# Rope keys padded to 128 rows and a bf16 mask product in the latent-attention scores of a two-block layer stack

## The chip, the cores and the metric

The kernel runs on one core of a Trainium2 chip. The metric is the time of one execution on the device, in microseconds (us). The engines are named as in the profile: PE is TensorE's matmul, PEld its weight load, DVE is VectorE, ACT is ScalarE, POOL is GpSimd, SP is SyncE, which issues DMAs here.

## What is computed

Two model blocks follow one another on 512 tokens of width 1024. The first has two layers: gated linear attention with a SwiGLU feed-forward, then latent attention (MLA) with another SwiGLU. The second block has pooling and convolution branches and a mixture of single-neuron experts. The change lies in the MLA layer, whose scores are

```
s = (einsum('bqhd,bkhd->bhqk', qn_b, k_nope)
     + einsum('bqhd,bkd->bhqk', qr_b, k_rope)).astype(float32) * scale
mask = kpos[None, :] <= qpos[:, None]
p = softmax(where(mask, s, -inf), axis=-1)
o = einsum('bhqk,bkhd->bqhd', p, v)
```

There are 8 heads, 128 non-rope and 64 rope dimensions, a value width of 128, and 4 blocks of 128 queries. The rope key `k_rope` is one for all heads. Everything is float32.

## The kernel before

The engines' programs are written out by hand and tied by semaphores; each engine runs its own list in order. Weights come from memory in blocks through a ring of four (`raw`, then ACT copies them into `w_hi`, L566, then POOL makes the rest `w_lo`, L548), and a dense product is three single-pass products of such parts. Stages run one after the other; PE's order is `pe_program`, and the MLA stage is `pe_mla`.

Within the MLA stage the latent projections come first, then the projections for queries, keys and values, then the score loop, then the output projection `mla_out` by dense products. The queries' rope parts are in `m_qr`, [128 partitions, 4, 512]: two heads share one slot, the even head in partitions 0 to 63, the odd one in 64 to 127. The rotated key `m_kr`, [128, 512], holds the same 64 rows twice, once in each half. DVE makes it at L1364 to L1366 (`kr_done`), long ahead of the score loop: ACT waits for `kr_done` at L822 before it writes `m_sw` again, and PE waits for it at L1881.

The score loop runs over s = 0 to 31, four steps for a head, with a query block `qb` = s % 4. Step s computes scores for n = 128 (qb + 1) keys, so 128, 256, 384 and 512 columns in turn:

- PE: three products accumulate in one bank `pa[:, s % 3]`: the non-rope part (L1890, `m_qn` by `m_kn`, 128 rows), the rope part (L1891, `m_qr` by `m_kr`, the 64 rows of the head's half), and the causal mask of the diagonal 128 columns (L1892, the identity by a table `causal_t` of 0 and -1e30). All operands are float32; one float32 product shows in the trace as two MATMUL records. Then come the transposes of the probabilities of step s - 2 (L1899), and once in a head, at qb = 2, the product of the transposed probabilities with the values of the head before (`m_PT` by `m_v`, eight records), "PV" below.
- DVE: the row maximum of step s (L1381), its scaling (L1382), then for step s - 1 the reciprocal of the sum (L1386) and the scaling of `m_P` (L1388, `at_n`), on which the transposes wait; once in a head `h_lo` (L1392).
- ACT: the exponential of step s (L854, `at_p`), the copy of the transposed probabilities of step s - 2 (L861, `at_To`), once in a head `h_hi` (L867).

PE's product helper is `mm` at L1623, so products of many stages have that one line in the profile and are told apart by their operands; the mask product is the one with `consts` alone. SP has loaded three blocks for `mla_out` before the loop starts, and `mla_out` waits for the last `h_lo` (L1910).

Of the kernel before, what the change touches and what calls it, by code (L numbers as in the profile page):

```python
# [24 lines left out]
BF16 = mybir.dt.bfloat16  # L25
U32 = mybir.dt.uint32
I32 = mybir.dt.int32
ALU = mybir.AluOpType
# [3 lines left out]
P = 128  # L32
S = 512
# [12 lines left out]
MH, NOPE, ROPE, MVD = 8, 128, 64, 128  # L46
# [101 lines left out]
def two_blocks(nc, A, out):  # L148
# [11 lines left out]
    def at(name, offset, shape, dt=F32):  # L160
        return nc.alloc_sbuf_tensor_at(name, [P] + shape, dt, offset=base + offset)

    K = 1024
# [14 lines left out]
    rstd_off = misc  # L178
    rstd = at("rstd", misc, [S])
    misc += 2 * K  # L180
    ada_off = misc
# [13 lines left out]
    def ar(name, offset, shape, dt=F32):  # L195
        n = int(np.prod(shape)) * (2 if dt == BF16 else 4)
        assert offset + n <= arena_bytes, (name, offset + n, arena_bytes)
        return at(name, AR + offset, shape, dt)
# [34 lines left out]
    m_qr = ar("m_qr", 16 * K, [MH // 2, S])  # L233
    m_kn = ar("m_kn", 24 * K, [MH, S])
    m_v = ar("m_v", 40 * K, [TT, MH * MVD])
    m_kr = ar("m_kr", 56 * K, [S])
    m_cos = ar("m_cos", 58 * K, [S])
    m_sin = ar("m_sin", 60 * K, [S])
    m_c = ar("m_c", 62 * K, [5, S])
    m_kraw = ar("m_kraw", 72 * K, [S])  # L240
    m_sw = ar("m_sw", 74 * K, [S])
    m_t = ar("m_t", 76 * K, [S])
# [5 lines left out]
    c_lo = ar("c_lo", 82 * K, [5, S], F32R)  # L248
    c_hi = at("c_hi", ada_off, [5, S], F32R)
    m_st = at("m_st", ada_off + 10 * K, [MH * TT, 4])  # L250

    ssq = ar("ssq", 0, [DT, S])
    s_a1 = ar("s_a1", 0, [4, S])
# [54 lines left out]
    pa = nc.alloc_psum_tensor("pa", [P, 4, 512], F32)  # L308
# [6 lines left out]
    def const(name, n, rows=P):  # L315
        return consts[0:rows, CONST[name]:CONST[name] + n]

    ident, ones = const("ident", P), const("ones", P)
# [34 lines left out]
    k_raw, sw_done, qr_done, kr_done = sem("k_raw"), sem("sw_done"), sem("qr_done"), sem("kr_done")  # L353
# [416 lines left out]
    def act_mla(act, hi):  # L770
# [42 lines left out]
        for t in range(12):  # L813
            m = M0["mla_q"] + t // 2
            hi.upto(m + 3)
            act.wait_ge(blk_done, m + 1)
            bank = ps[:, (T + t) % RING, :]
            if t < MH:
                nc.scalar.activation(m_qn[:, t, :], bank, ACT.Copy).then_inc(tile_free, 1)
            else:  # L820
                j = t - MH
                act.wait_ge(kr_done, 1)  # L822
                if j >= 2:
                    act.wait_ge(qr_done, j - 1)
                dst = (m_sw, m_kraw)[j % 2]
                for q in range(4):
                    nc.scalar.activation(dst[32 * q:32 * q + 32, :], bank[32 * (q ^ 1):32 * (q ^ 1) + 32, :], ACT.Copy)\
                      .then_inc(sw_done, 1)
# [502 lines left out]
    def dve_mla(dve):  # L1331
        def step(ins):
            own_d.link(dve, ins)

        v = nc.vector

        dve.wait_ge(ld_v[2], 16)
        step(v.tensor_copy(m_ang[:, :], m_pos[:, :]))
        step(v.tensor_scalar(m_ang[:, :], m_ang[:, :], const("freq", 1), None, ALU.mult))
        step(v.tensor_scalar(m_t[:, :], m_ang[:, :], 1.0 / TWO_PI, MAGIC, ALU.mult, ALU.add))  # L1340
        step(v.tensor_scalar(m_t[:, :], m_t[:, :], -MAGIC, None, ALU.add))
        for c in (C1, C2, C3):
            step(v.scalar_tensor_tensor(out=m_ang[:, :], in0=m_t[:, :], scalar=-c, in1=m_ang[:, :], op0=ALU.mult, op1=ALU.add))

        step(v.tensor_scalar(m_t[:, :], m_ang[:, :], np.pi / 2, None, ALU.add))
        step(v.tensor_scalar(m_cos[:, :], m_t[:, :], PI_BELOW, -TWO_PI, ALU.is_gt, ALU.mult))
        step(v.tensor_tensor(m_t[:, :], m_t[:, :], m_cos[:, :], ALU.add))
        step(v.tensor_scalar(m_t[:, :], m_t[:, :], PI_BELOW, -PI_BELOW, ALU.min, ALU.max))
        v.tensor_scalar(m_ang[:, :], m_ang[:, :], PI_BELOW, -PI_BELOW, ALU.min, ALU.max).then_inc(ang_done, 1)

        dve.wait_ge(trig_done, 1)
        for a, tiles in enumerate((range(0, 3), range(3, 5))):
            dve.wait_ge(c_rs, a + 1)
            for t in tiles:
                g = col("mla_g_q", t) if t < 3 else col("mla_g_kv", t - 3)
                v.scalar_tensor_tensor(out=m_c[:, t, :], in0=m_c[:, t, :], scalar=g, in1=m_rs[:, a, :],
                                       op0=ALU.mult, op1=ALU.mult).then_inc(c_t, 1)
            for t in tiles:
                dve.wait_ge(c_h, t + 1)
                v.tensor_tensor(c_lo[:, t, :], m_c[:, t, :], c_hi[:, t, :].bitcast(F32), ALU.subtract).then_inc(c_rd, 1)  # L1360

        dve.wait_ge(trig_done, 1)
        dve.wait_ge(tile_free, T0["mla_qn"])
        step(v.tensor_tensor(m_kr[:, :], m_kraw[:, :], m_cos[:, :], ALU.mult))  # L1364
        step(v.tensor_tensor(m_sw[:, :], m_sw[:, :], m_sin[:, :], ALU.mult))
        v.tensor_tensor(m_kr[:, :], m_kr[:, :], m_sw[:, :], ALU.add).then_inc(kr_done, 1)  # L1366
        T = T0["mla_qr"]
        for j in range(MH // 2):
            dve.wait_ge(blk_done, M0["mla_q"] + 4 + j // 2 + 1)
            dve.wait_ge(sw_done, 4 * (j + 1))  # L1370
            sw = (m_sw, m_kraw)[j % 2]
            v.tensor_tensor(m_qr[:, j, :], m_cos[:, :], ps[:, (T + j) % RING, :], ALU.mult).then_inc(tile_free, 1)
            step(v.tensor_tensor(sw[:, :], sw[:, :], m_sin[:, :], ALU.mult))
            dve.wait_ge(tile_free, T + j + 1)
            v.tensor_tensor(m_qr[:, j, :], m_qr[:, j, :], sw[:, :], ALU.add).then_inc(qr_done, 1)

        n_it = MH * TT
        for s in range(n_it + 4):
            if s < n_it:
                dve.wait_ge(at_s, s + 1)  # L1380
                step(v.tensor_reduce(m_st[:, s, 0:1], pa[:, s % 3, 0:P * (s % TT + 1)], AX.X, ALU.max))  # L1381
                v.tensor_scalar(m_st[:, s, 1:2], m_st[:, s, 0:1], -MSCALE, None, ALU.mult).then_inc(at_m, 1)  # L1382
            if 1 <= s <= n_it:
                r = s - 1
                dve.wait_ge(at_p, s)
                step(v.reciprocal(m_st[:, r, 3:4], m_st[:, r, 2:3]))  # L1386
                pr = m_P[:, r % 2, 0:P * (r % TT + 1)]
                v.tensor_scalar(pr, pr, m_st[:, r, 3:4], None, ALU.mult).then_inc(at_n, 1)  # L1388
            if s >= 7 and (s - 7) % TT == 0:
                h = (s - 7) // TT  # L1390
                dve.wait_ge(at_oh, h + 1)
                v.tensor_tensor(h_lo[:, h, :], ps[:, 2 + h % 2, :], h_hi[:, h, :].bitcast(F32), ALU.subtract).then_inc(at_ol, 1)  # L1392
        dve_residual(dve, "mla_out", 1, 2, 3)
# [228 lines left out]
    def mm(out, a, b, start, stop_):  # L1622
        return nc.tensor.matmul(out, a, b, start=start, stop=stop_)  # L1623
# [209 lines left out]
    def pe_mla(pe):  # L1833
# [44 lines left out]

        pe.wait_ge(tile_free, T0["mla_out"])
        pe.wait_ge(qr_done, MH // 2)  # L1880
        pe.wait_ge(kr_done, 1)  # L1881
        n_it = MH * TT
        for s in range(n_it + 3):
            if s < n_it:
                h, qb = divmod(s, TT)
                if s >= 3:
                    pe.wait_ge(at_p, s - 2)
                n, q = P * (qb + 1), slice(qb * P, (qb + 1) * P)
                half = slice(ROPE * (h % 2), ROPE * (h % 2 + 1))
                mm(pa[:, s % 3, 0:n], m_qn[:, h, q], m_kn[:, h, 0:n], True, False)  # L1890
                mm(pa[:, s % 3, 0:n], m_qr[half, h // 2, q], m_kr[half, 0:n], False, False)  # L1891
                mm(pa[:, s % 3, n - P:n], ident, const("causal_t", P), False, True).then_inc(at_s, 1)  # L1892
            if 2 <= s < n_it + 2:
                r = s - 2
                pe.wait_ge(at_n, r + 1)
                if r >= 2:
                    pe.wait_ge(at_To, r - 1)
                for kb in range(r % TT + 1):
                    last = nc.tensor.transpose(ps[:, r % 2, kb * P:(kb + 1) * P], m_P[:, r % 2, kb * P:(kb + 1) * P], ident)  # L1899
                last.then_inc(at_T, 1)  # L1900
            if s >= 6 and (s - 6) % TT == 0:
                h = (s - 6) // TT
                pe.wait_ge(at_To, TT * (h + 1))
                if h >= 2:
                    pe.wait_ge(at_ol, h - 1)
                for kb in range(TT):
                    last = mm(ps[:, 2 + h % 2, kb * P:S], m_v[:, kb, h * MVD:(h + 1) * MVD], m_PT[:, h % 2, kb, kb * P:S],
                              kb == 0, kb == TT - 1)
                last.then_inc(at_o, 1)
# [251 lines left out]
```

## Time and profile before

| | us |
|---|---|
| median of 3 runs | 3251.67 (3250.89 to 3251.94) |
| the profiled execution, its own time | 3249.77 |
| its span, first to last instruction | 3247.7 |
| PE busy | 3108.9 (96%) |
| POOL, DVE, ACT busy | 1771, 1606, 1152 |
| score loop, first score product to the first `mla_out` product | 808.98 to 903.73 |

```text
span 3247.7 us, 44125 instructions
## 1 busy us (share of the span) xinstructions
PE 3108.9 (96%) x14602; PEld 2502.0 (77%) x14602; DVE 1605.6 (49%) x2785; ACT 1151.8 (35%) x1478; POOL 1771.1 (55%) x2040
## 2 busy tenths in 40 slices
PE   5988999999999999997999999999999999999998
PEld 3777788876578887775788888888888788888886
DVE  7873454322435551694407996444411444444443
ACT  4354322236332213433323325555543322232222
POOL 3833677645047766573455665444446665566663
PEclk8989999999999999998999999999999999999999
DMA  7511455423025553221233444555564655555652
GB/s 304 207 36 61 151 186 191 153 71 96 1 78 200 187 187 112 87 88 61 85 98 112 146 136 169 184 184 184 188 240 141 217 200 186 179 169 196 202 191 72
DMA packets 170201, 481.94 MB, mean 148 GB/s; under 512 B 15360, under 2 KB 48896, under 8 KB 168080
## 3 DMA queue, kind: packets, MB, share of 16 engines
q1 hardware_dynamic: 147680, 410.83, 38.8%
q10 hardware_dynamic: 22448, 70.14, 5.6%
q8 instruction: 46, 0.75, 0.1%
q14 instruction: 27, 0.22, 0.0%
HBM read 411.70 MB, written 69.21 MB: 148 GB/s over the span
## 4 chain that ended last, share of the span: by engine, by line
PE 56%; issue 21%; POOL 19%; DVE 2%; ACT 1%; DMA 0%; DVEq 0%; POOLq 0%; SPq 0%; ACTq 0%
PE ps L1623 52%; POOL w_lo L548 19%; PE pa L1623 3%; DVE s_acc L1417 1%; DMA e_g<-expert_act 0%; DVEq L1414 0%; DVE s_pb L1429 0%; DVE s_tmp L1468 0%; DVE mg_lo L1470 0%; ACT mg_hi L918 0%; DVE s_m L1466 0%; DVE x L1122 0%; ACT L614 0%; POOLq L546 0%; POOLq L552 0%
## 5 line engine op out<-in xcount | busy, mean ns | idle before, releaser
L548 POOL TENSOR_TENSOR w_lo<-raw,w_hi 128x256 fp32r<-128x256 f32 x2036 | 1770.9, 902 | 1446.4 <-ACT w_hi L566 1444.5
L1623 PE MATMUL ps<-h_hi,w_hi 128*128 128x512 f32 x2392 | 950.2, 397 | 43.2 <-POOL w_lo L548 19.6
L1623 PE MATMUL ps<-h_hi,w_lo 128*128 128x512 f32 x2392 | 939.7, 393 | 0.0
L1623 PE MATMUL ps<-h_lo,w_hi 128*128 128x512 f32 x2392 | 915.7, 390 | 0.0
L566 ACT ACTIVATE w_hi<-raw 128x1024 fp32r<-128x1024 f32 x509 | 538.8, 1060 | 844.4 <-PE ps L1623 727.9
L1623 PEld LDWEIGHTS ps<-h_hi,w_hi 128*128 128x128 f32 x2392 | 454.9, 190 | 145.2 <-issue 25.9
L1623 PEld LDWEIGHTS ps<-h_hi,w_lo 128*128 128x128 f32 x2392 | 454.6, 190 | 95.3
L1623 PEld LDWEIGHTS ps<-h_lo,w_hi 128*128 128x128 f32 x2392 | 450.3, 188 | 93.3 <-issue 1.7
L1623 PE MATMUL ps<-wa_hi,w_lo 128*128 128x512 f32 x1024 | 408.6, 399 | 0.0
L1623 PE MATMUL ps<-wa_lo,w_hi 128*128 128x512 f32 x1024 | 403.5, 394 | 0.0
L1623 PE MATMUL ps<-wa_hi,w_hi 128*128 128x512 f32 x1024 | 401.5, 392 | 0.3 <-DVE x L1587 0.3
L1069 DVE CUSTOM_DVE_ANT_0 ada<-ada,cvec 128x1024 f32<-128x1024 f32 x144 | 228.5, 1625 | 32.1 <-DMA ada<-in_ada 27.9
L1623 PEld LDWEIGHTS ps<-wa_lo,w_hi 128*128 128x128 f32 x1024 | 192.2, 188 | 50.1
L1623 PEld LDWEIGHTS ps<-wa_hi,w_hi 128*128 128x128 f32 x1024 | 192.2, 188 | 46.5 <-DVE x L1587 0.7
L1623 PEld LDWEIGHTS ps<-wa_hi,w_lo 128*128 128x128 f32 x1024 | 192.2, 188 | 44.2
L1580 DVE TENSOR_TENSOR wa_lo<-e_t,wa_hi 128x512 fp32r<-128x512 f32 x128 | 137.5, 1074 | 152.6 <-ACT wa_hi L1005 152.6
L925 ACT ACTIVATE g_act<-ps 128x512 f32<-128x512 f32 x128 | 76.6, 598 | 348.9 <-PE ps L1623 348.9
L1577 DVE TENSOR_TENSOR e_t<-e_g,e_w 128x512 f32<-128x512 f32 x128 | 108.5, 848 | 165.1 <-DMA e_g<-expert_act 164.4
L1587 DVE SCALAR_TENSOR_TENSOR x<-ps,mod,x 128x512 f32<-128x512 f32 x128 | 95.7, 748 | 183.7 <-PE ps L1623 183.6
L1005 ACT ACTIVATE wa_hi<-e_t 128x512 fp32r<-128x512 f32 x128 | 80.8, 631 | 207.2 <-DVE e_t L1577 207.2
L1552 DVE TENSOR_TENSOR oh_hit<-iota_t,r_key 128x1024 bf16<-128x1024 bf16 x64 | 46.5, 726 | 215.5 <-PE pa L1623 215.1
L985 ACT ACTIVATE w_st<-pa 128x512 f32<-128x512 f32 x128 | 134.2, 1160 | 39.3 <-PE pa L1623 30.5
(315 smaller groups left out, 3088.7 us busy)
## 6 DMA issues: line engine op xcount, KB each, us to landing
ada<-in_ada SPq DMA_DIRECT2D x144, 512.0 KB, 4.4
raw<-in_expert_u SPq DMA_DIRECT2D x128, 512.0 KB, 4.1
raw<-in_expert_v SPq DMA_DIRECT2D x128, 512.0 KB, 4.2
raw<-in_ffn_in SPq DMA_DIRECT2D x88, 512.0 KB, 3.5
expert_act<-g_act ACTq DMA_DIRECT2D x128, 256.0 KB, 4.3
gate_matrix<-w_st ACTq DMA_DIRECT2D x16, 2048.0 KB, 6.7
e_w<-gate_matrix SPq DMA_DIRECT2D x16, 2048.0 KB, 11.2
e_g<-expert_act SPq DMA_DIRECT2D x128, 256.0 KB, 7.8
```

What stands on the lines that cost most here:

```text
L548: last = nc.gpsimd.tensor_tensor(w_lo[:, k, c:c + 256], raw[:, k, c:c + 256], w_hi[:, k, c:c + 256].bitcast(F32), ALU.subtract)
L566: nc.scalar.activation(w_hi[:, k, :], raw[:, k, :], ACT.Copy).then_inc(hi_done, 1)
L925: nc.scalar.activation(g_act[:, k % 2, :], ps[:, (T + k) % RING, :], ACT.Gelu_apprx_tanh)\
L985: nc.scalar.activation(w_st[:, b, :, 4 * q:4 * q + 4].rearrange("p n t -> p t n"), pa[:, q % 4, :].rearrange("p (t n) -> p t n", t=4), ACT ...
L1005: nc.scalar.activation(wa_hi[:, b, k, :], e_t[:, :], ACT.Copy).then_inc(wa_h, 1)
L1069: return nc.vector.tensor_tensor_reduce(out=w, in0=w, in1=cvec[:, :], scale=1.0, scalar=0.0, op0=ALU.mult, op1=ALU.add, accum_out=dst).the ...
L1417: v.scalar_tensor_tensor(out=s_acc[:, t, :], in0=s_gl[:, t, bass.ds(i + 1, S)], scalar=cols[:, bass.ds(i + (COLS["dw_kernel"] + t * CK + 1 ...
L1552: v.tensor_tensor(oh_hit[:, b, :, :, :], column, key1, ALU.is_equal).then_inc(oh_hits, 1)
L1577: v.tensor_tensor(e_t[:, :].rearrange("p (t k) -> p t k", k=WTOK), e_g[:, k % 4, :].rearrange("p (t k) -> p t k", k=WTOK), e_w[:, :, k, :] ...
L1580: v.tensor_tensor(wa_lo[:, b, k, :], e_t[:, :], wa_hi[:, b, k, :].bitcast(F32), ALU.subtract).then_inc(wa_done, 1)
L1587: v.scalar_tensor_tensor(out=x[:, k, :], in0=ps[:, (T + k) % RING, :], scalar=mod[:, GATE[6] + k:GATE[6] + k + 1], in1=x[:, k, :], op0=ALU ...
L1623: return nc.tensor.matmul(out, a, b, start=start, stop=stop_)
```

## The change

`m_kr` becomes two tensors, one for the even and one for the odd heads. Each has the rotated key in the 64 partitions of its heads and zeros in the other 64. The second lies where `rstd` lies, which is free in this stage. The rope product then takes all 128 rows of `m_qr`: the other head's rows meet zeros. The identity and the mask table are copied once to bf16 (0 and 1 are exact, and -1e30 stays as good as minus infinity), into unused bytes beside `m_st`, and the mask product uses these. DVE now issues two multiplications, two memsets, two half-height additions and two casts where it issued two multiplications and one addition, and `kr_done` counts six of them; ACT at L822 and PE at L1881 wait for all six.

```diff
-    m_kr = ar("m_kr", 56 * K, [S])
+    m_kr = [ar("m_kr0", 56 * K, [S]), at("m_kr1", rstd_off, [S])]
...
+    ident_b = at("ident_b", ada_off + 10 * K + 512, [P], BF16)
+    causal_b = at("causal_b", ada_off + 10 * K + 768, [P], BF16)
...
-                act.wait_ge(kr_done, 1)
+                act.wait_ge(kr_done, 6)
...
-        step(v.tensor_tensor(m_kr[:, :], m_kraw[:, :], m_cos[:, :], ALU.mult))
+        step(v.tensor_tensor(m_t[:, :], m_kraw[:, :], m_cos[:, :], ALU.mult))
         step(v.tensor_tensor(m_sw[:, :], m_sw[:, :], m_sin[:, :], ALU.mult))
-        v.tensor_tensor(m_kr[:, :], m_kr[:, :], m_sw[:, :], ALU.add).then_inc(kr_done, 1)
+        for a in range(2):
+            mine, other = slice(ROPE * a, ROPE * (a + 1)), slice(ROPE * (1 - a), ROPE * (2 - a))
+            v.memset(m_kr[a][other, :], 0.0).then_inc(kr_done, 1)
+            v.tensor_tensor(m_kr[a][mine, :], m_t[mine, :], m_sw[mine, :], ALU.add).then_inc(kr_done, 1)
+        v.tensor_copy(ident_b[:, :], ident).then_inc(kr_done, 1)
+        v.tensor_copy(causal_b[:, :], const("causal_t", P)).then_inc(kr_done, 1)
...
-        pe.wait_ge(kr_done, 1)
+        pe.wait_ge(kr_done, 6)
...
-                half = slice(ROPE * (h % 2), ROPE * (h % 2 + 1))
                 mm(pa[:, s % 3, 0:n], m_qn[:, h, q], m_kn[:, h, 0:n], True, False)
-                mm(pa[:, s % 3, 0:n], m_qr[half, h // 2, q], m_kr[half, 0:n], False, False)
-                mm(pa[:, s % 3, n - P:n], ident, const("causal_t", P), False, True).then_inc(at_s, 1)
+                mm(pa[:, s % 3, 0:n], m_qr[:, h // 2, q], m_kr[h % 2][:, 0:n], False, False)
+                mm(pa[:, s % 3, n - P:n], ident_b[:, :], causal_b[:, :], False, True).then_inc(at_s, 1)
```

## Rows read from the trace of the kernel before

**Rows 1.** Windows: stretch; its length, then PE, PEld, DVE, ACT, POOL busy, clock.

```profile
779.00:782.40 3.40, 1.84 (x7) 1.05 (x6) 2.26 (x4) 3.28 (x6) 2.69 (x4) 1.00 0.02 5
809.80:820.00 10.20, 10.20 (x20) 4.49 (x19) 2.52 (x10) 1.86 (x7) 0.00 (x0) 0.50 0.01 2
894.00:898.40 4.40, 1.79 (x12) 1.07 (x11) 2.49 (x7) 2.14 (x5) 0.00 (x0) 1.00 0.00 0
898.40:902.00 3.60, 3.60 (x7) 1.83 (x7) 0.00 (x0) 0.00 (x0) 0.00 (x0) 0.53 0.00 0
```

**Rows 2.** Timeline, PE alone, in one head: start, us, line, product, count, idle before.

```profile
828.87 1.02 PE L1623 MATMUL pa<-m_kn,m_qn 128*128 128x512 f32 x2
829.82 1.12 PE L1623 MATMUL pa<-m_kr,m_qr 64*128 64x512 f32 x2
830.88 0.49 PE L1623 MATMUL pa<-consts 128*128 128x128 f32 x2
831.20 0.38 PE L1899 MATMUL ps<-consts,m_P 128*128 128x128 f32 x2
831.42 0.39 PE L1623 MATMUL pa<-m_kn,m_qn 128*128 128x128 f32 x2
831.74 0.48 PE L1623 MATMUL pa<-m_kr,m_qr 64*128 64x128 f32 x2
832.15 0.49 PE L1623 MATMUL pa<-consts 128*128 128x128 f32 x2
832.87 0.55 PE L1899 MATMUL ps<-consts,m_P 128*128 128x128 f32 x3 [0.23 <-DVE m_P L1388]
833.25 0.60 PE L1623 MATMUL pa<-m_kn,m_qn 128*128 128x256 f32 x2
...
834.73 0.60 PE L1899 MATMUL ps<-consts,m_P 128*128 128x128 f32 x4
...
837.18 2.32 PE L1623 MATMUL ps<-m_PT,m_v 128*128 128x512 f32 x8
839.34 0.59 PE L1623 MATMUL pa<-m_kn,m_qn 128*128 128x512 f32 x1
```

**Rows 3.** Timeline of the same head, DVE and ACT.

```profile
831.40 0.69 DVE L1381 TENSOR_REDUCE m_st<-pa 128x1 f32<-128x512 f32 x1 [3.39 <-PE pa L1623]
...
832.39 0.42 DVE L1388 TENSOR_SCALAR m_P<-m_P,m_st 128x384 f32<-128x384 f32 x1
...
833.90 0.49 DVE L1388 TENSOR_SCALAR m_P<-m_P,m_st 128x512 f32<-128x512 f32 x1
...
836.04 0.59 ACT L861 ACTIVATE m_PT<-ps 128x512 f32<-128x512 f32 x1
```

**Rows 4.** Timeline, PE alone, in the expert stage, where bf16 products stand between others.

```profile
1999.94 1.55 PE L1623 MATMUL pa<-oh_gate,oh_key 128*128 128x128 bf16 x24
2001.29 0.48 PE L1623 MATMUL ps<-h_hi,w_hi 128*128 128x512 f32 x1
2001.61 0.39 PE L1623 MATMUL ps<-h_lo,w_hi 128*128 128x512 f32 x1
2001.84 0.40 PE L1623 MATMUL ps<-h_hi,w_lo 128*128 128x512 f32 x1
```

**Rows 5.** Timeline, DVE alone, around `m_kr`, and a memset from the groups by line.

```profile
761.61 1.12 DVE L1366 TENSOR_TENSOR m_kr<-m_kr,m_sw 128x512 f32<-128x512 f32 x1
776.20 0.69 DVE L1372 TENSOR_TENSOR m_qr<-m_cos,ps 128x512 f32<-128x512 f32 x1 [13.47 <-ACT m_sw L827]
...
L1157 DVE MEMSET g_attn<- 128x2048 f32 x1 | 1.8, 1765 | 1.2 <-PEq L2156 1.2
```

**Rows 6.** Timeline, PE alone, start of the loop and its last PV.

```profile
810.48 1.06 PE L1623 MATMUL pa<-m_kn,m_qn 128*128 128x256 f32 x2
...
813.20 1.49 PE L1623 MATMUL pa<-m_kn,m_qn 128*128 128x384 f32 x2
...
898.20 4.12 PE L1623 MATMUL ps<-m_PT,m_v 128*128 128x512 f32 x8 [0.69 <-ACT m_PT L861]
```

## The prediction

> **What bounds the kernel now.** The page comes first: PE is busy 96% of the span and no other engine above 55%, so the time is PE's list and the gaps in it. The change touches only the score loop of the MLA stage, 808.98 to 903.73, so I read the views of that stretch. The timeline of PE alone over one head [rows 2] shows a head period of 10.47 us (828.87 to 839.34) with one visible wait, the 0.23 us before the transposes of the 384-column step; those wait for DVE's scaling of `m_P`. The reader should see that PE's list fills the head, and that DVE's chain comes just behind it at one place. The windows [rows 1] show the second thing: from 809.8 to 820 TensorE was granted its lower level, 1.2 GHz (clock 0.50), though PE has work without a break. The third view, DVE alone ahead of the loop [rows 5], tells whether the added DVE work has room.
>
> **The rope product.** The yardstick is PV in [rows 2]: eight records over 2560 columns take 837.18 to 839.34, 2.16 us, so 0.84 ns for a column of a record when one 128-row float32 product follows another. By it the two records of the non-rope product and the two of the rope product cost 4 x 128 x 0.84 = 0.43 us for 128 columns, 0.86 for 256, 1.30 for 384 and 1.73 for 512. Measured from the first product to the transposes, or to the end of the mask product at its 0.32 us: the 512-column step 828.87 to 831.20, 2.33; the 128-column step 831.42 to 832.15 plus 0.32, 1.05; the 256-column step 833.25 to 834.73, 1.48 [rows 2]. The excess is 0.60, 0.62 and 0.62 us, independent of the columns, so I take 0.61 for 384 columns as well. Within it the mask product is two records of 128 columns, 0.22 at the yardstick. The other 0.39 us stands at the two borders of the rope product (64 rows between 128 and 128): it takes 1.06 us where the non-rope one with the same columns takes 0.95, and 0.41 against 0.32. Streaming 128 rows in place of 64 costs nothing, as columns are what is counted: 512 columns cost 1.06 us even with 64 rows.
>
> The Trainium skill's page TensorEngine Tiling, section Key Properties, says that a change of tiling mode drains the engine. By that rule the borders are the cause and vanish with equal heights; the page gives no price. Were the rule wrong here, the 0.39 us would belong to every change of weights, and rival B would hold; PV in [rows 2], which changes weights for every column block with no such gap, speaks for the rule.
>
> **The mask product.** In bf16 it is one record of 128 columns. Twenty-four such products take 1999.94 to 2001.29, 1.35 us, 0.06 each [rows 4]. At the return to other operands one product takes 0.32 where the next takes 0.23 (2001.29, 2001.61, 2001.84), 0.09 more. So the mask product costs between 0.06 and 0.15 us; the trace has none in a float32 group. I take 0.12, nearer the upper end, since each is alone between float32 work here. **PE's list thus shrinks by 0.61 - 0.12 = 0.49 us a step,** 15.7 over 32 steps if nothing else bound it.
>
> **What DVE's chain takes back, in one head.** (1) After the 512-column step. Now: mask product 830.88, maximum from 831.40, scaling of the 384 columns 832.39 for 0.42, transposes 832.87 [rows 2, 3]; 1.99 us from mask to transposes, in which PE works 0.32 + 0.22 + 1.05 = 1.59. With the mask product 0.20 shorter the chain starts 0.20 sooner and takes 1.79; PE's work is 0.12 + 0.22 + 0.55 = 0.89 and PE waits 0.9. Gain 0.20, not 0.69. (2) The next transposes come 1.86 us later (832.87 to 834.73), and DVE is ready at 833.90 + 0.49 + 0.05 = 834.44, 1.57 after. PE's work falls to 0.38 + 0.86 + 0.12 = 1.36, so the chain decides: gain 0.29. (3) From there to PV now 2.45 us (834.73 to 837.18); 0.49 less is 1.96, while PV needs ACT's copy, 836.04 + 0.59 = 836.63, 1.90 after [rows 3]. That just holds: gain 0.49. (4) PV and the first two products of the 512-column step: gain 0.60 - 0.32 = 0.28. Sum 1.26 us a head, and the period goes from 10.47 to 9.21.
>
> **First head, last head.** At 1.2 GHz the 256-column step takes 810.48 to 813.20, 2.72 us [rows 6]; at twice the yardstick it would be 1.72 + 0.2, so the gain is 0.8, and over the first three steps and the 512-column step up to its mask about 2.7. Seven periods follow: 7 x 1.26 = 8.8. The last mask product gives 0.2; behind it the chain of waits to the first `mla_out` product, 10 us, is untouched. Sum 11.7. As head 1 begins sooner, more of it falls into the slow clock if that ends at 820 as now, which returns about 0.6: **11.1 us with the slow stretch as it is.**
>
> **The clock.** The slow stretch at the loop's start lasts 10.2 us; the one at the last PV, all of 128 rows, is over by 902, after 3.6 us, though both have PE busy throughout [rows 1]. What stands in the first and not in the second are the 64-row products, nearly half of PE's time there, and the gaps at their borders. Both go. I expect the loop to be at 2.4 GHz after a stretch like the second, so some 6.6 us less at half speed: 3.3 us of PE work, less 0.7 for the DVE wait of point 1, which now shows in head 1 as well. Gain 2.6.
>
> **DVE ahead of the loop.** The addition of `m_kr` ends at 762.7, and DVE then sits idle 13.47 us until 776.20, waiting for ACT [rows 5]. Added are two memsets of 512 columns, one more addition, two casts of 128 columns. A memset of 2048 columns takes 1.77 us, so one of 512 under 0.5; an addition 1.12. With the casts bounded by an addition each, at most 0.9 + 1.1 + 2.2 = 4.2 us. The idle time hides it; ACT's wait at L822 stands before the copies that end with the row at 776.20, nine us after DVE is through, and PE's comes at 809. Queued behind these operations on DVE is only the work from 776.20, and POOL's `w_lo` in this stretch is a possible loser if the memsets slow it, bounded by the 0.4 us that the addition itself lost to company (1.12 against 0.69). Cost 0, at most 0.4. Were that cover gone, 4.2 us would come straight onto the stage. No DMA is added or moved.
>
> **Sum.** 11.1 + 2.6 = 13.7. The profiled execution took 3249.77, so 3236.1 for it; the median of the runs is 1.90 higher, so **3238.0 us**.
>
> **Rivals.** A, the slow stretch stays as long as now: gain 11.1, 3240.6. For it: nothing in one trace proves what ends it. B, the change does not remove the gaps, as they belong to the change of weights and not of height: only the mask product gains, 0.20 x 32 = 6.4, so 3245.3; PV speaks against it. C, the chain bites deeper than I read: point 3 has 0.06 us of room, and if ACT's copy is late by 0.3 in each of 7 heads and point 2 gains nothing (7 x 0.29), the gain is 13.7 - 2.1 - 2.0 = 9.6, 3242.1. D, the slower side: PE now waits 1.1 us in each 9.21 (12%), and the clock falls within heads. At 1.2 GHz each head's 8.1 us of work doubles; the gain of 13.7 is used up once 27 us of the loop run at half speed, and at half speed throughout it would be 3238.0 + 7 x 8.1 = 3294.7. [...] Against it here: from 779 to 782.4 PE was busy 1.84 of 3.40 us and the clock stayed 1.00; it fell after 894 to 898.4, with 1.79 of 4.40 [rows 1]. No stretch of the new head is that empty.
>
> **How the numbers follow.** Chances: forecast 0.56, A 0.24, B 0.06, C 0.06, D 0.03, others 0.05. Range: below, a mask product at 0.06 gives 0.9 more, and the last PV, which spends 4.12 us at the lower level where PV elsewhere takes 2.32 [rows 2, 6], may fall into the full clock, 1.8 more: 3235.3, so 3235.0. Above, A with a mask product of 0.15 (0.6) and one more such slow piece (1.8): 3243.0, which also holds C. B and D stay out. A measurement of this kernel tells about 0.2%, 6.5 us, from no change, so the border is 3245.2: faster 0.91 (forecast, A, C, part of B and the others), same 0.06, slower 0.03.
>
> **What would show it.** In the changed kernel's trace, start to start: the rope product should take the same 0.84 ns a column as its neighbour, with its weight load ahead of its end; the mask product 0.06 to 0.15; a head 9.2 us, with waits of 0.9 and 0.2 us before the transposes of the 384- and 512-column steps, ended by DVE's scaling; the clock at full level by about 814; DVE's new work over by 767. The loop should last 94.75 - 13.7 = 81 us. The prediction is wrong if the rope product keeps its extra 0.1 us and the mask's start its 0.1 (B), if the wait before PV grows (C), or if the clock reads below 1.00 inside heads (D).

## The result and the profile after

The changed kernel takes 3232.8 us, the median of four executions (3228.7 to 3237.5), against 3251.8 (3250.9 to 3255.8) for the kernel before beside it: a ratio of 0.9935, 95% interval 0.9921 to 0.9949. That is faster, as forecast, but 2.2 us below the low end of the range. Its profiled execution took 3233.8 us with a span of 3231.9. In further executions the changed kernel had medians of 3237.3 (6) and 3235.1 (7). All 17 together have a median of 3234.5 (3228.7 to 3244.4), 50 of the kernel before 3251.8 (3242.7 to 3266.2): 17.3 us, of which the score loop, as the traces show, holds 16.4.

The timeline of PE alone over one head of the changed kernel answers [rows 2]:

```profile
828.00 2.33 PE L1630 MATMUL ps<-m_PT,m_v 128*128 128x512 f32 x8
830.16 1.02 PE L1630 MATMUL pa<-m_kn,m_qn 128*128 128x512 f32 x2
831.02 1.02 PE L1630 MATMUL pa<-m_kr,m_qr 128*128 128x512 f32 x2
831.88 0.22 PE L1630 MATMUL pa<-causal_b,ident_b 128*128 128x128 bf16 x1
831.93 0.39 PE L1905 MATMUL ps<-consts,m_P 128*128 128x128 f32 x2
832.16 0.39 PE L1630 MATMUL pa<-m_kn,m_qn 128*128 128x128 f32 x2
832.38 0.39 PE L1630 MATMUL pa<-m_kr,m_qr 128*128 128x128 f32 x2
832.61 0.22 PE L1630 MATMUL pa<-causal_b,ident_b 128*128 128x128 bf16 x1
833.60 0.55 PE L1905 MATMUL ps<-consts,m_P 128*128 128x128 f32 x3 [0.77 <-DVE m_P L1395]
...
835.17 0.66 PE L1905 MATMUL ps<-consts,m_P 128*128 128x128 f32 x4
...
837.13 2.33 PE L1630 MATMUL ps<-m_PT,m_v 128*128 128x512 f32 x8
839.29 0.59 PE L1630 MATMUL pa<-m_kn,m_qn 128*128 128x512 f32 x1
```

Read it by starts. From 830.16 the non-rope product takes 0.86 us and the rope product 0.86, equal and at 0.84 ns a column; before it was 0.95 and 1.06. The mask product takes 0.05 to 0.06 us (831.88 to 831.93) where it took 0.32. The head period is 9.13 us (830.16 to 839.29) after 10.47. Of that PE now waits, from start to start, 0.94 us at 832.66 and about 0.27 before 835.17, 1.21 us together. By the same count the one wait of [rows 2] was 0.40 us (832.47 to 832.87; its record shows 0.23, as it counts from the record's end).

The two waits end with DVE's scaling of `m_P`, as the timeline of DVE in the same head shows beside [rows 3]:

```profile
832.14 0.69 DVE L1388 TENSOR_REDUCE m_st<-pa 128x1 f32<-128x512 f32 x1 [2.85 <-PE pa L1630]
...
833.12 0.42 DVE L1395 TENSOR_SCALAR m_P<-m_P,m_st 128x384 f32<-128x384 f32 x1
833.46 0.68 DVE L1399 TENSOR_TENSOR h_lo<-ps,h_hi 128x512 fp32r<-128x512 f32 x1
...
834.06 0.28 DVE L1388 TENSOR_REDUCE m_st<-pa 128x1 f32<-128x128 f32 x1
...
834.63 0.49 DVE L1395 TENSOR_SCALAR m_P<-m_P,m_st 128x512 f32<-128x512 f32 x1
```

The windows (length, then PE, PEld, DVE, ACT, POOL busy, clock, DMA) of the slow stretch at the loop's start and of the rest of the loop, of which [rows 1] had 10.2 us at 0.50:

```profile
807.50:810.90 3.40, 3.40 (x12) 2.49 (x12) 0.94 (x5) 0.46 (x2) 0.00 (x0) 0.51 0.01 2
810.90:885.60 74.70, 64.67 (x294) 39.86 (x292) 38.49 (x133) 35.58 (x103) 0.00 (x0) 1.00 0.01 2
```

The stretch at 1.2 GHz is 3.4 us long, and the last PV, at 898.20 in [rows 6] for 4.12 us at the lower level, now takes 2.42 us at 2.4 GHz, as PE's timeline at the loop's end shows:

```profile
877.54 0.22 PE L1630 MATMUL pa<-causal_b,ident_b 128*128 128x128 bf16 x1
877.60 0.39 PE L1905 MATMUL ps<-consts,m_P 128*128 128x128 f32 x2
879.26 0.55 PE L1905 MATMUL ps<-consts,m_P 128*128 128x128 f32 x3 [1.27 <-DVE m_P L1395]
880.45 0.66 PE L1905 MATMUL ps<-consts,m_P 128*128 128x128 f32 x4 [0.64 <-DVE m_P L1395]
881.79 2.42 PE L1630 MATMUL ps<-m_PT,m_v 128*128 128x512 f32 x8 [0.69 <-ACT m_PT L863]
885.63 0.50 PE L1630 MATMUL ps<-h_hi,w_hi 128*128 128x512 f32 x1 [1.41 <-DVE h_lo L1399]
```

The loop, from its first score product at 807.30 to 885.63, takes 78.3 us after 94.75. The spans differ by 15.8: ahead of the loop the changed kernel is 1.7 us earlier, behind it 2.3 longer. The rest of this document takes up what in the loop was mis-sized, and what lies outside it. In it "stretch" is a piece of time at 1.2 GHz, and a "border" a place at which a product of 64 rows follows one of 128 or the other way round.

### The profile page after: what moved, and what is told of

It reads as the page before. It is cut to its first block, busy times and chain, and to the rows that moved or that the text cites. A ratio compares the mean times of both kernels' runs of the same rounds, so it can differ in the third digit from the quotient of the medians.

```text
span 3231.9 us, 44066 instructions
## 1 busy us (share of the span) xinstructions
PE 3085.9 (95%) x14570; PEld 2494.6 (77%) x14570; DVE 1609.3 (50%) x2790; ACT 1151.8 (36%) x1478; POOL 1775.5 (55%) x2040
## 4 chain that ended last, share of the span: by engine, by line
PE 68%; issue 14%; POOL 10%; DVE 5%; ACT 1%; DMA 1%; DVEq 0%; POOLq 0%; SPq 0%; ACTq 0%
PE ps L1630 63%; POOL w_lo L550 10%; PE pa L1630 5%; DVE ada L1071 1%; DVE s_acc L1424 1%; DMA ada<-in_ada 1%; DMA e_g<-expert_act 0%; DVEq L1421 0%; DVE g_qs L1218 0%; DVE s_pb L1436 0%; DVE g_ks L1219 0%; DVE s_tmp L1475 0%; ACT w_hi L568 0%; DVE mg_lo L1477 0%; DVE g_b L1195 0%
## 5 line engine op out<-in xcount | busy, mean ns | idle before, releaser
L1630 PE MATMUL ps<-wa_hi,w_hi 128*128 128x512 f32 x1024 | 408.5, 399 | 0.6 <-DVE x L1594 0.6
L927 ACT ACTIVATE g_act<-ps 128x512 f32<-128x512 f32 x128 | 76.6, 599 | 348.9 <-PE ps L1630 348.9
L1594 DVE SCALAR_TENSOR_TENSOR x<-ps,mod,x 128x512 f32<-128x512 f32 x128 | 95.6, 747 | 181.1 <-PE ps L1630 180.9
L1154 DVE SCALAR_TENSOR_TENSOR x<-ps,mod,x 128x512 f32<-128x512 f32 x40 | 29.8, 750 | 239.3 <-PE ps L1630 239.3
```

The lines of the kernel that those rows point to most:

```text
L927: nc.scalar.activation(g_act[:, k % 2, :], ps[:, (T + k) % RING, :], ACT.Gelu_apprx_tanh)\
L1154: nc.vector.scalar_tensor_tensor(out=x[:, k, :], in0=ps[:, (T + k) % RING, :], scalar=mod[:, GATE[n] + k:GATE[n] + k + 1], in1=x[:, k, :], ...
L1594: v.scalar_tensor_tensor(out=x[:, k, :], in0=ps[:, (T + k) % RING, :], scalar=mod[:, GATE[6] + k:GATE[6] + k + 1], in1=x[:, k, :], op0=ALU ...
```

## The experiments

The first four tell the parts of the change apart, and the scatter of the whole.

### The rope part alone

```diff
-                mm(pa[:, s % 3, n - P:n], ident_b[:, :], causal_b[:, :], False, True).then_inc(at_s, 1)
+                mm(pa[:, s % 3, n - P:n], ident, const("causal_t", P), False, True).then_inc(at_s, 1)
```

> The padded 128-row rope product is kept, the mask product is float32 again. My theory (the gap at the borders of the 64-row product is 0.39 us a step; those products also keep TensorE at its lower level): no border left, so a mask product of two records at 0.11 each, 0.22 us; a head of 9.13 + 0.28 = 9.4 us, a slow stretch of about 3.4 us at the loop's start as in the changed kernel, a loop of 80 to 82 us (before 94.75, changed 78.33), time about 3237. Rival B (gaps belong to any change of weights): a head of about 10.2 us, time about 3247. Rival for the clock (the bf16 mask ended the slow stretch): it stays at 10.2 us, loop 83 to 84.

Measured: 3238.1 us (3236.4 to 3241.5, 4 executions), ratio to before 0.9954 (0.9936 to 0.9972); loop 81.1 us, head 9.46. PE's timeline in one head:

```profile
831.33 1.02 PE L1630 MATMUL pa<-m_kn,m_qn 128*128 128x512 f32 x2
832.19 1.02 PE L1630 MATMUL pa<-m_kr,m_qr 128*128 128x512 f32 x2
833.05 0.38 PE L1630 MATMUL pa<-consts 128*128 128x128 f32 x2
833.27 0.38 PE L1905 MATMUL ps<-consts,m_P 128*128 128x128 f32 x2
833.49 0.39 PE L1630 MATMUL pa<-m_kn,m_qn 128*128 128x128 f32 x2
```

The rope product takes 0.86 us after 1.06, and the unchanged float32 mask product falls from 0.32 to 0.22 just by standing behind a product of its own height. The slow stretch is 3.4 us (807.7 to 811.1). So the padding alone gives 13.6 of the loop's 16.4 us, and the mask did not shorten the stretch. About 1.7 of the 13.6 us are the last PV, which took 2.42 us here too. All that was expected of this run came out; rival B and the rival for the clock fall.

### The mask part alone

```diff
-                mm(pa[:, s % 3, 0:n], m_qr[:, h // 2, q], m_kr[h % 2][:, 0:n], False, False)
+                half = slice(ROPE * (h % 2), ROPE * (h % 2 + 1))
+                mm(pa[:, s % 3, 0:n], m_qr[half, h // 2, q], m_kr[h % 2][half, 0:n], False, False)
```

> The mask product in bf16 is kept, the rope product reads the 64 rows of its head again. My theory: the borders stay, the mask product falls from 0.32 to 0.07 to 0.16 us, the step by about 0.2, the head from 10.47 to 9.9, and the slow stretch at the loop's start stays at 10.2 us, as the 64-row products cause it; loop 89 to 90 us, time about 3246. Rival (the slow stretch was shortened by the mask): it is 3.4 us and the loop 86 to 87, time about 3243.

Measured: 3247.6 us (3243.2 to 3252.5, 10), ratio 0.9985 (0.9974 to 0.9997); loop 91.0, head 9.73. The mask product takes 0.07 us, the low end of what was expected, though it still follows a 64-row product. The head came out 0.17 shorter than expected, the loop 1 to 2 us longer, and the cause of the latter is in the windows:

```profile
807.40:824.50 17.10, 17.10 (x41) 7.62 (x40) 5.78 (x22) 4.80 (x16) 0.00 (x0) 0.50 0.00 1
824.50:892.70 68.20, 62.75 (x255) 32.33 (x256) 33.11 (x113) 29.83 (x87) 0.00 (x0) 1.00 0.00 1
```

With the 64-row product kept, the stretch at 1.2 GHz grew from 10.2 to 17.1 us; I had expected 10.2. That less 128-row work now stands between the 64-row products is a possible reason, not a tested one. Either way the mask product did not shorten it.

### DVE's part alone

All three products as before, DVE's list as in the changed kernel (both edits above together).

> DVE makes both padded keys and both bf16 tables, but all three score products are as before. My theory: nothing, loop 94.7 us, time within 0.5 us of before, as DVE's work lies in 13.5 us of idle time. Rival (part of the 19.0 us between the medians comes from a shift of the work ahead of the loop, not from the loop, whose own gain is 16.4): 2 to 3 us faster than before.

Measured: 3254.5 us (3247.1 to 3262.1, 10), ratio 1.0007 (0.9992 to 1.0022); loop 94.64, slow stretch 10.2. The added DVE work costs nothing that can be measured: the interval alone would leave room for some us, but the loop is as before. The work is over at 765.0, 9.55 us before DVE's next work, as DVE's timeline in the changed kernel shows; the additions cost 1.2 us each although they have half the rows, and the six operations take 4.9 us (760.07 to 764.98) where the one addition took 1.1:

```profile
760.07 0.48 DVE L1370 MEMSET m_kr<- 64x512 f32 x1 [0.17 <-DVE m_sw L1367]
760.58 1.16 DVE L1371 TENSOR_TENSOR m_kr<-m_t,m_sw 64x512 f32<-64x512 f32 x1
761.80 0.48 DVE L1370 MEMSET m_kr<- 64x512 f32 x1
762.32 1.27 DVE L1371 TENSOR_TENSOR m_kr<-m_t,m_sw 64x512 f32<-64x512 f32 x1
763.62 0.66 DVE L1372 CAST ident_b<-consts 128x128 bf16<-128x128 f32 x1
764.20 0.78 DVE L1373 CAST causal_b<-consts 128x128 bf16<-128x128 f32 x1
774.53 0.69 DVE L1379 TENSOR_TENSOR m_qr<-m_cos,ps 128x512 f32<-128x512 f32 x1 [9.55 <-ACT m_sw L829]
```

### The changed kernel again

> The changed kernel again, for its scatter. Its four times spread over 8.8 us, 3228.7 to 3237.5, those of before over 4.9. My theory: the 2.6 us between 19.0 (medians) and 16.4 (the loop in the two profiles) are scatter outside the loop; the median of more runs is at 3234 to 3236 and the loop 78.3, or 80.1 where the last PV falls into the slow clock. Rival: the gain outside the loop is real, the median stays at 3233 or below.

Measured: 3237.3 us (3232.4 to 3244.4, 6), ratio 0.9953 (0.9937 to 0.9969); beside it 23 executions of the kernel before spread from 3242.9 to 3261.1. The loop is 78.3 again. The median came out above what either theory gave; as the loop is the same, the difference lies outside it, and there is more of it than I had allowed for.

The next four test the mechanisms.

### Height or change of height

```diff
+                half = slice(ROPE * (h % 2), ROPE * (h % 2 + 1))
-                mm(pa[:, s % 3, 0:n], m_qn[:, h, q], m_kn[:, h, 0:n], True, False)
-                mm(pa[:, s % 3, 0:n], m_qr[:, h // 2, q], m_kr[h % 2][:, 0:n], False, False)
+                mm(pa[:, s % 3, 0:n], m_qn[half, h, q], m_kn[half, h, 0:n], True, False)
+                mm(pa[:, s % 3, 0:n], m_qr[half, h // 2, q], m_kr[h % 2][half, 0:n], False, False)
```

> The changed kernel with 64 rows in both the non-rope and the rope product, in the same rows; half of the contraction of the non-rope part is left out, so the scores are others. Columns are the same. My theory (the cost is at a change of height, not in 64 rows): non-rope to rope runs at 0.84 ns a column without a gap, and 0.1 us each appears in front of the non-rope product and between rope and mask product. The slow stretch at the start of the loop is longer than the 17.1 us of the run with one 64-row product. Rival: 64-row products are slow wherever they stand, so both gaps stay inside; rival for the clock: the stretch is 3.4 us as in the changed kernel, since the gaps and not the rows set it.

This kernel leaves out half of the contraction of the non-rope part, so its scores are not the reference's; only its times are read. Measured in one execution, 3252.1 us: loop 90.7 us, head 9.73, the same as with one 64-row product. PE's timeline:

```profile
834.25 1.12 PE L1630 MATMUL pa<-m_kn,m_qn 64*128 64x512 f32 x2
835.22 1.02 PE L1630 MATMUL pa<-m_kr,m_qr 64*128 64x512 f32 x2
836.17 0.23 PE L1630 MATMUL pa<-causal_b,ident_b 128*128 128x128 bf16 x1
836.23 0.39 PE L1906 MATMUL ps<-consts,m_P 128*128 128x128 f32 x2
836.55 0.48 PE L1630 MATMUL pa<-m_kn,m_qn 64*128 64x128 f32 x2
836.88 0.38 PE L1630 MATMUL pa<-m_kr,m_qr 64*128 64x128 f32 x2
837.19 0.23 PE L1630 MATMUL pa<-causal_b,ident_b 128*128 128x128 bf16 x1
```

The weight loads (PEld) of the non-rope and the rope product in this kernel, and that of the rope product in the kernel before:

```profile
834.25 0.29 PEld L1630 LDWEIGHTS pa<-m_kn,m_qn 64*128 64x128 f32 x2
834.79 0.19 PEld L1630 LDWEIGHTS pa<-m_kr,m_qr 64*128 64x128 f32 x1 [0.24 <-issue]
```

```profile
829.82 0.29 PEld L1623 LDWEIGHTS pa<-m_kr,m_qr 64*128 64x128 f32 x2 [0.76 <-issue]
```

Twice as many 64-row products, and no more loss: the cost is at the change of height. The non-rope product now takes 0.97 us and the rope product 0.95 in place of 1.06. A product behind a border starts together with its weight load (834.25 here, 829.82 before), while the rope product, which no longer stands behind one, has its load 0.43 us ahead of its start. There are still two borders a step. The product ahead of each takes 0.1 us longer (the rope product 0.95 against 0.86, the transposes at 836.23 0.32 against 0.22). Behind the first the float32 product takes 0.11 us longer; behind the second the bf16 mask, whose load is short, takes 0.06 to 0.07 us, next to nothing more, where the float32 mask of the kernel before took 0.10 more. So a border costs about 0.2 us with a float32 product behind it and about 0.1 with the bf16 mask behind it: 0.3 us a step in this run and in the one with the mask part alone, 0.39 before. That explains the head of 9.73 us in that run. The Trainium skill's page TensorEngine Tiling, section Key Properties, says of a changed tiling mode that it drains the engine. The trace agrees, with 0.1 us lost ahead of each border, and adds the price. The clock part of the expectation was missed: the stretch is 17.1 us, as in the run with one 64-row product and not longer, so its length doesn't simply follow the share of 64-row products.

### PV moved into the wait

PE waits 1.21 us a head for DVE's chain. If that is so because too little PE work stands behind the 128-column scores, PV can be put there, ahead of the transposes of its step. ACT's `h_hi` moves by two steps with it, and DVE's `h_lo` from s >= 7 to s >= 9:

```diff
...
-            if s >= 6 and (s - 6) % TT == 0:
-                h = (s - 6) // TT
+            if s >= 8 and (s - 8) % TT == 0:
+                h = (s - 8) // TT
...
```

> The changed kernel with PV of a head moved from behind the transposes of its successor's 128-column step to the place between the 128-column scores of the next head but one and the transposes of the 384-column step, where PE now waits 0.99 us for DVE; the copies h_hi and h_lo move with it, and so leave DVE's chain between the two waits. My theory (what DVE's chain took back is 0.99 + 0.27 us a head, because too little PE work stands there): both waits go, a head of 9.13 becomes 7.8 to 8.0 us, the loop 69 to 71 us, time 8 us under the changed kernel. Rival (DVE or ACT is the bound of a head, wherever PV stands): other waits open and the head stays above 8.8.

Measured: 3229.6 us (3225.2 to 3236.7, 5), ratio 0.9923 (0.9893 to 0.9952); head 7.87, loop 68.7, a little under what was expected. PE's timeline has no wait left within a head:

```profile
835.27 0.39 PE L1630 MATMUL pa<-m_kn,m_qn 128*128 128x128 f32 x2
835.50 0.39 PE L1630 MATMUL pa<-m_kr,m_qr 128*128 128x128 f32 x2
835.72 0.22 PE L1630 MATMUL pa<-causal_b,ident_b 128*128 128x128 bf16 x1
835.77 2.38 PE L1630 MATMUL ps<-m_PT,m_v 128*128 128x512 f32 x8
837.99 0.49 PE L1914 MATMUL ps<-consts,m_P 128*128 128x128 f32 x3
```

The chain's price, 9.13 - 7.87 = 1.26 us a head, is thereby measured, and it was one of placement. (That the forecast's gain for a head is 1.26 us as well is chance.) Of this price 0.40 us stood there before the change. Without its waits PE's list for a head went from 10.07 to 7.92 us, 2.15 less; 1.34 of that came through, and the chain kept 0.81.

### Work in the gap ahead of the loop

```diff
+        for _ in range(2):
+            mm(pa[:, 3, :], ones, consts[:, 0:512], True, True)
         pe.wait_ge(tile_free, T0["mla_out"])
```

> The changed kernel with two products of constants (128 rows, 512 columns, float32, result unused) in the 2.15 us in which PE waits for ACT's copies of m_v ahead of the loop. My theory (this idle time is what brings the slow stretch at the loop's start): the clock stays at 1.00 there, and the loop takes 1.7 us less, 76.6 measured from its first score product. Rival: the stretch starts all the same, as PE was half idle before it as well (779 to 803).

Measured: 3236.7 us (3232.6 to 3243.6, 7), ratio 0.9950 (0.9928 to 0.9972); loop 78.93. The windows show why not 76.6:

```profile
800.00:879.40 79.40, 71.00 (x323) 44.72 (x322) 38.73 (x135) 37.95 (x109) 2.83 (x4) 1.00 0.04 13
879.40:889.60 10.20, 8.10 (x19) 5.02 (x17) 0.69 (x1) 2.14 (x3) 2.81 (x4) 0.50 0.15 51
```

The slow stretch at the start is gone, here and in both profiles of the next section, which shows that PE's 2.15 us of idling brought it; up to the last mask product the loop is 1.7 us shorter (68.58 after 70.24), as expected. But in this profile the clock fell in the gaps at the loop's end, where in the changed kernel it had not, and there 10.2 us at 1.2 GHz cost more: from the last mask product to `mla_out` it took 10.35 us in place of 8.09 (last PV 4.63 us). Half the expectation held; the rival was wrong too.

### Both, and more executions

> Both, PV moved and the two products of constants. Theory: the gains add, loop 67.5 to 69.5 us, time 9 to 10 us under the changed kernel, if the slow stretches behind the loop don't grow by as much. Rival: the clock falls later instead, and the sum stays at that of PV moved alone.

Measured: 3224.7 us (3222.0 to 3229.9, 4), ratio 0.9911 (0.9877 to 0.9945); loop 67.0, all at 2.4 GHz, 0.5 us under the low end of what was expected. The gains add.

> PV moved and the two products of constants again, in more executions. Theory: the loop is 67.0 us as in the first run, 11.3 under the changed kernel's 78.33; the medians differ by 9 to 12 us. Rival: the clock or the convolution stage takes it back and they differ by less than 6.

Measured: 3222.8 us (3220.1 to 3227.8, 6), ratio 0.9910 (0.9890 to 0.9930); loop 67.0 again. The median is 12.3 us under that of the changed kernel beside it, just over the expected 9 to 12. The ten together have a median of 3223.5, 11 us under the changed kernel's: this version beats both.

> The changed kernel a third time, for its median against that of before in more executions. The two medians so far are 3232.8 and 3237.3, those of before 3251.8 and 3252.2. In two of ten profiles the convolution stage far behind the loop takes about 10 us longer, because one w_lo on POOL stands still for some 30 us beside DVE's convolution, and the changed kernel's part behind the loop is 1.3 to 2.3 us longer for another half-speed stretch. My theory: such scatter outside the loop lies over a gain of 16.4 in the loop, and the median difference is 14 to 18 us. Rival: the 19.0 of the first four executions holds, from a gain outside the loop.

Measured: 3235.1 us (3233.6 to 3243.0, 7), ratio 0.9950 (0.9931 to 0.9969), loop 78.3; the median of the kernel before beside it was 3250.3, 15.2 more, as expected. The 19.0 of the first four did not hold.

The scatter has one source that I could see. In the profile of the run with the filler, one of POOL's `w_lo` instructions in the convolution stage stands for 40.8 us beside DVE's convolution; PE waits 29 us for it, and the stage takes 9.4 us more (from its first `s_mix` product to its first `s_acc` product 76.5 against 67.1). The instruction stands from 1417.40 to 1458.20, and DVE works without a break from 1414.91 to 1457.62. PV moved alone shows the same, with 77.1 us; the changed kernel's three profiles don't, nor do the two with both edits. First the run with the filler, then the changed kernel (durations in ns, least, median, most):

```profile
L550 POOL TENSOR_TENSOR w_lo<-raw,w_hi x18: 717/736/40801, 1417.4 to 1469.8; 128x256 fp32r<-128x256 f32 x18
...
  PE ps L1630: 29.3, 1
```

```profile
L550 POOL TENSOR_TENSOR w_lo<-raw,w_hi x28: 739/1182/1262, 1417.2 to 1452.4; 128x256 fp32r<-128x256 f32 x28
```

Neither edit touches this stage, and with both of them it takes its 67.1 to 67.2 us, so the mode seems to come and go by execution; each kernel was profiled once in a run, so this is not shown for one and the same kernel. Whether the slowest executions of the kernel before are of this mode was not seen, as none of them was profiled.

## Why the prediction was wrong

Two steps failed. In the sum for the loop the last PV was left at its slow 4.12 us, a term of nothing; it took 2.42. And the scatter of the whole kernel, outside the loop, was given no share of the range. The mechanisms were right. The loop's gain was put at 13.7 us and is 16.4. By pieces, with the terms as they stood in the sum (the first piece ran from 808.98 to 830.88 and now from 807.30 to 822.74, the last from 893.68 to 903.73 and now from 877.54 to 885.63):

| | forecast | measured |
|---|---|---|
| first score product to the mask of the second head's 512-column step | 2.7 - 0.6 + 2.6 + 1.26 = 5.96 | 21.90 - 15.44 = 6.46 |
| six further head periods | 6 x 1.26 = 7.6 | 6 x 1.34 = 8.0 |
| last mask product to `mla_out` | 0.2 | 10.05 - 8.09 = 1.96 |

**The borders: right.** 0.39 us a step, and they vanish with equal heights; three runs agree (rope alone, mask alone, both at 64 rows).

**The mask product: right in kind, mis-sized.** I took 0.12 between bounds of 0.06 and 0.15, nearer the upper. It is 0.06, the value inside the run of bf16 products in [rows 4]; the 0.09 that the return to wide operands costs there does not appear, neither with transposes behind the mask product nor with PV (835.72 to 835.77 in the run with PV moved). Why it stands in [rows 4] is open. The one-record product also releases DVE sooner. Together: head 9.13 in place of 9.21, a wait of 0.94 in place of 0.9 and of 0.27 in place of 0.2; about 0.5 us over the periods.

**DVE's chain: right.** Points 1 to 4 gave transposes 1.79, 1.57 and PV 1.96 us after the one before; measured 1.72, 1.57, 1.96. PV moved shows that the waits were this chain's.

**The clock at the start: right, with its cause.** 3.4 us in place of 10.2, and the padding alone does it. Rival A falls. The first piece, in which this gain lies, was put 0.5 us too low.

**The last PV: the step that failed in the sum.** The piece behind the last mask product was put at 0.2 us of gain, "untouched" but for the mask, and gained 1.96. Of that 1.7 us are the last PV, 4.12 us before and 2.42 now. I counted them as a lucky end of the range instead of asking what the new timing does to it. It took 3.97 to 4.12 us in all four profiles with 64-row products in the loop, and 2.42 in seven of the eight with padded keys, the three of the changed kernel among them. The eighth is the filler's, with 4.63. So the 64-row products bear on it, as on the stretch at the start, but the padding alone does not secure it. What decides it in the filler's run stays open.

**The level of the whole: the step that failed for the range.** With 16.4 the forecast would have been 3235.3, just what I had given as the lowest case, and still above the measured 3232.8. The rest, 2.5 us to the first median and 0.8 to that of all 17, lies outside the loop. I read three executions within 1.05 us of each other as the kernel's scatter and gave none of the range to it. Fifty executions of the kernel before spread over 23.5 us, and profiles of kernels that are alike ahead of the loop begin it anywhere from 806.7 to 814.0. Behind the loop the changed kernel has 6.8 us at half speed at 933.9 where the one before had 3.4 at 953.0; in its second profile it is about as long, in its third 3.4. A range of 8 us on a gain of 14 needed at least 3 us more at either side.

**No cost on DVE, no slow clock within heads: right.** DVE's added work is 3.8 us, within the bound of 4.2, and hidden; 13% of waiting in each head left the clock at 1.00 (window 810.90 to 885.60), so rival D falls.

## What to carry to other kernels

A product over half of the rows costs as many columns as a full one, and when it stands alone between full ones it costs two borders besides: pad it to full height with zeros if the zeros can be made in idle time, or put products of equal height side by side. When PE's list shrinks, follow each wait one step further: here a chain on DVE left PE 1.26 us of waiting in each head, and moving a product that was already there into the gap won it back. And take a kernel's scatter from many executions before giving a range of a few microseconds.

## What the runs showed of the hardware that was not expected

- A border between 64-row and 128-row float32 products costs about 0.2 us, 0.1 ahead of the change and 0.1 behind it, whatever the columns (0.95 and 1.06 against 0.86 us at 512 columns, 0.32 and 0.41 against 0.22 at 128). With a bf16 product of 128 columns behind it the second 0.1 us all but goes (0.07 us against 0.05 to 0.06).
- With PE busy throughout, the stretch at 1.2 GHz after the 2.15 us gap lasts 3.4 us when all products have 128 rows (the changed kernel and the rope part alone), 10.2 with the 64-row rope and float32 mask (two profiles), 17.1 with the bf16 mask and one or both score products at 64 rows (one profile each). PE's busy share in the profile does not tell these apart.
- Filling the gap takes that stretch away (three profiles), and in one of them another stood at the loop's end (10.2 us at 879.4).
- One `w_lo` of 128x256 on POOL can stand for 40.8 us, until just after DVE's unbroken work ends, against 1.2 us in another execution of the same stage.
